# The overflow loop of an expert stage moved to the middle of the experts, and four reorderings in the r/k/v stage

## What is computed

```python
xs = cols + (prev - cols) * rwkv_mu            # r, k, v and three low-rank inputs
kk = (k * k_k) / max(norm of each head of (k * k_k), 1e-12)
k  = k * (1.0 + (a - 1.0) * k_a)
g  = sigmoid(g_d) @ g_lora_up                  # g_d: 128 of the columns
bonus = sum over a head of (r * k * r_k), times v
...
grp = argmax(x2d @ router_group + router_group_bias)
top_v, top_i = top_k(expert scores inside the group, 2)
for e in range(N_EXPERTS):                     # 32 experts, D_EXPERT = 256
    h = silu(x2d @ moe_w_gate[e]) * (x2d @ moe_w_up[e])
    y = y + combine[:, e:e + 1] * (h @ moe_w_down[e])
y = rms_norm(x + y)
```

## Time and profile before

| | us |
|---|---|
| median of 3 runs | 1114.06 |
| lowest, highest | 1112.53, 1117.73 |
| the profiled execution | 1116.11 |
| its span, first to last instruction | 1114.4 |

### The profile page before, as it was taken

How to read it: one execution, slowest core, us unless ns; L and a number is a source line. 1 busy time by engine, 2 the same in 40 slices (tenths; PEclk the granted TensorE clock), 3 DMA queues, 4 the chain that set the end, 5 groups by cost and what they waited for, 6 DMA issues and landing times. The chain is left out here.

```text
span 1114.4 us, 24781 instructions
## 1 busy us (share of the span) xinstructions
PE 1014.4 (91%) x10429; PEld 768.3 (69%) x10429; DVE 566.8 (51%) x1195; ACT 365.2 (33%) x783; POOL 442.8 (40%) x458
## 2 busy tenths in 40 slices
PE   5999999789999999999999999999976999888784
PEld 5777777578888887888888888884554555454441
DVE  6577777556565643777645446333363222211126
ACT  3444544545545443444244450000111111110112
POOL 7646546244554424977653335410001222211110
PEclk9999999899999999999999999999987999988998
DMA  8022221110000007541242224407786999999975
GB/s 257 18 78 73 69 81 38 37 47 4 4 5 4 4 4 190 164 112 37 63 143 85 76 66 161 151 1 288 318 338 223 414 415 414 415 418 416 416 293 229
DMA packets 84935, 183.11 MB, mean 164 GB/s; under 512 B 9921, under 2 KB 59613, under 8 KB 76122
## 3 DMA queue, kind: packets, MB, share of 16 engines
q1 hardware_dynamic: 78173, 168.59, 41.6%
q0 software_dynamic: 5168, 8.56, 2.1%
q10 hardware_dynamic: 1485, 4.39, 1.0%
HBM read 173.24 MB, written 17.55 MB: 171 GB/s over the span
## 5 line engine op out<-in xcount | busy, mean ns | idle before, releaser
L2802 DVE SCALAR_TENSOR_TENSOR ex_sg<-tl_psA,ex_slot_rs,ex_sg 128x128 f32<-128x128 f32 x32 | 11.2, 351 | 138.3 <-ACT ex_sg L2602 138.1
L2294 POOL DMA_INDIRECT d_y<-tl_xn,ex_sidx x32 | 31.9, 998 | 118.6 <-DVE tl_xn L2806 108.5
L2289 POOL DMA_INDIRECT tl_xn<-d_tok,ex_gidx x17 | 17.9, 1051 | 148.4 <-DVEq L2794 76.4
L262 PE MATMUL psv<-xT,w_sum 128*128 128x260 f32 x256 | 61.6, 384 | 0.9 <-DVE uv_gu L1595 0.6
L224 POOL TENSOR_TENSOR w_sum<-w 128x512 f32<-128x512 f32 x16 | 21.2, 1324 | 94.0 <-PE mg_w L262 93.8
L262 PEld LDWEIGHTS psv<-xT,w_sum 128*128 128x128 f32 x256 | 48.4, 190 | 9.4 <-issue 1.0
L2602 ACT ACTIVATE ex_sg<-tl_psA,ex_slot_rs 128x128 f32<-128x128 f32 x32 | 11.8, 368 | 130.9 <-PE tl_psA L2460 130.9
L1058 PE MATMUL ck_b<-ck_X,ck_V 64*64 64x64 f32 x1280 | 50.4, 222 | 4.1 <-issue 3.3
L262 PE MATMUL rk_ps<-xT,rk_w 128*128 128x260 f32 x208 | 50.1, 384 | 0.0
L262 PE MATMUL rk_ps<-xS,rk_w 128*128 128x260 f32 x200 | 48.6, 386 | 0.0
L1058 PEld LDWEIGHTS ck_b<-ck_X,ck_V 64*64 64x64 f32 x1280 | 43.0, 134 | 4.5 <-issue 4.2
(11 more groups left out here) (615 smaller groups left out, 2795.2 us busy)
## 6 DMA issues: line engine op xcount, KB each, us to landing
wd<-in_moe_w_down SPq DMA_DIRECT2D x15, 1024.0 KB, 23.4
rk_w<-in_w_in SPq DMA_DIRECT2D x12, 1024.0 KB, 5.5
tl_x<-in_moe_w_down SPq DMA_DIRECT2D x9, 1024.0 KB
w_uv<-in_w_in SPq DMA_DIRECT2D x16, 512.0 KB, 5.2
w<-in_w_in SPq DMA_DIRECT2D x8, 1024.0 KB, 5.8
xT<-in_moe_w_gate SPq DMA_DIRECT2D x5, 1024.0 KB
xT<-in_moe_w_up SPq DMA_DIRECT2D x5, 1024.0 KB
bonus_all<-in_moe_w_gate SPq DMA_DIRECT2D x5, 1024.0 KB
```

Source lines behind the costliest of these rows:

```text
L262: ins = eng.matmul(bank[:, 0:TH], w[:, k, :], x[:, k, :], start=(first and k == 0), stop=(last and k == NK // 2 - 1), skip_group_check=True)
L2289: eng.indirect_dma_start(out=xg[:, p % 2, :], out_offset=None, in_=m.d_tok, in_offset=bass.IndirectOffsetOnAxis(ap=gidx[:, p:p + 1], axis= ...
L2294: eng.indirect_dma_start(out=m.d_y2, out_offset=bass.IndirectOffsetOnAxis(ap=rows, axis=0), in_=yo[:, x, :], in_offset=None, bounds_check= ...
L2802: eng.scalar_tensor_tensor(out=sg[:, out, :], in0=psg[out][:, P:2 * P], scalar=scale, in1=sg[:, out, :], op0=ALU.mult, op1=ALU.mult).then_ ...
```

## The change

In the r/k/v stage: (a) on VectorE the second `shift_mix` stands behind `u2(0)` instead of ahead of it; the tanh for `gate_in` stands behind `decays(1)` on ScalarE, the affine step of `gate_in` behind the weight sums of set 1 on GpSimd, and `keys(1)` waits for the tanh. (b) In the last set `head_sums(7)` stand behind the fourth product, `products(7)` ahead of `norms(6)`, `norms(7)` ahead of `c22`. (c) `roots(6)` stands behind `logs(7)`. (d) `scaled(6)` stands behind `c21`.

In the expert stage the loop stands at position 21 of 32 and has max number + 1 passes: its first pass is expert 31, the others are the overflow blocks. The positions are: 0 to 19 experts 0 to 19, position 20 expert 30, position 21 the loop, positions 22 to 31 experts 20 to 29. The loop's slot is 21 % 7 = 0. It has its own semaphores (`l_...`). The list of gathers is written in six instructions instead of two, because the pairs are no longer in the order of the experts.

```diff
-SPARE = 26 % SLOTS
+MID = 21
+SPARE = MID % SLOTS
 # GpSimd, r/k/v
-            eng.wait_ge(s_lt, 1)
-            eng.tensor_scalar(m.gate_in[:, :], m.gate_in[:, :], 0.5, 0.5, ALU.mult, ALU.add).then_inc(s_lt, 1)
-            eng.wait_ge(s_lt, 2)
...
                 weight_sums(eng, rkv_blocks(m, w, s), s_wsum, 4 * s)
+                if s == 1:
+                    eng.wait_ge(s_lt, 1)
+                    eng.tensor_scalar(m.gate_in[:, :], m.gate_in[:, :], 0.5, 0.5, ALU.mult, ALU.add).then_inc(s_lt, 1)
 # TensorE, r/k/v
-                if s % 3 == 2 and s < RKV_SETS - 1:
-                    head_sums(p)
+                if s % 3 == 2:
+                    head_sums(p if s < RKV_SETS - 1 else p + 1)
...
                 product(eng, bank_w, b.t1, x.s1, last=False).then_inc(s_prod, 1)
...
-                if s % 3 == 2:
+                if s % 3 == 2 and s < RKV_SETS - 1:
                     head_sums(p + 1)
 # ScalarE, r/k/v
                 decays(p + 1)
+                if i == 0:
+                    eng.wait_ge(s_xs, 2)
+                    eng.activation(m.gate_in[:, :], xs[:, 1, :], ACT.Tanh, scale=0.5).then_inc(s_lt, 1)
...
                 logs(p)
-                if i == NP // 2 - 1:
-                    roots(p)
                 kept_sums(p + 1)
                 logs(p + 1)
-                if i < NP // 2 - 1:
-                    roots(p)
+                roots(p)
                 roots(p + 1)
 # VectorE, r/k/v
                 u2(s)
+                if i == 0:
+                    low_rank_rows(1)
...
                 received(p + 1)
+                products(p + 1)
                 if i == NP // 2 - 1:
                     norms(p)
-                products(p + 1)
                 u3(s + 2)
+                norms(p + 1 if i == NP // 2 - 1 else p)
+                c22(s + 2)
                 if i < NP // 2 - 1:
-                    norms(p)
-                c22(s + 2)
-                norms(p + 1)
-                if i == NP // 2 - 1:
-                    scaled(p)
+                    norms(p + 1)
                 c21(s + 2)
             p, s = NP - 2, RKV_SETS - 1
+            scaled(p)
             c12(s)
             scaled(p + 1)
 # experts
+def counted(k):
+    return k if k <= MID else k - 1
+def expert_at(k):
+    return k if k < MID - 1 else k + NE - MID - 1 if k <= MID else k - 2
+def loads_at(k):
+    return k // SLOTS + (0 if k > MID and (k - MID) % SLOTS == 0 else 1)
 # SP
+            def load_block(k):
+                if k == MID + SLOTS:
+                    eng.wait_ge(l_over, 1)
+                else:
+                    eng.wait_ge(s_gu, counted(k - SLOTS) + 1)
+                load_gate_up(eng, m, a, k % SLOTS, expert_at(k))
+                if k != MID + SLOTS:
+                    eng.wait_ge(s_down, counted(k - SLOTS) + 1)
+                load_down(eng, m, a, k % SLOTS, expert_at(k))
+
+            for k in range(SLOTS, MID):
+                load_block(k)
             n = passes(eng)
             with eng.Fori(0, n) as q:
                 e = eng.value_load(m.block_expert[0:1, bass.ds(q, 1)], min_val=0, max_val=NE - 1)
                 eng.wait_ge(s_gu_free, q + 1)
-                load_gate_up(eng, m, a, SPARE, e)
+                load_gate_up(eng, m, a, SPARE, e, l_wgu)
                 eng.wait_ge(s_d_free, q + 1)
-                load_down(eng, m, a, SPARE, e)
+                load_down(eng, m, a, SPARE, e, l_wd)
+            for k in range(MID + 1, NE):
+                load_block(k)
 # TensorE
+                eng.wait_ge(l_wgu, q * 32 + 32)
+                gate_up(SPARE, 0, halves_of[1], 1, l_gu)
+                eng.wait_ge(l_h, q + 1)
+                turn_h(1, l_ht)
+                eng.wait_ge(l_hte, q + 1)
+                eng.wait_ge(l_wd, q * 16 + 16)
+                down(SPARE, 1, l_down)
+                eng.wait_ge(l_in, q * 16 + 16)
+                turn(0, l_t)
+                eng.wait_ge(l_yo, q + 1)
+                eng.wait_ge(l_xgT, q * 2 + 2)
+            up_block(MID + 1)
+            up_block(MID + 2, MID // 2 + 2, MID + 1)
+            for k in range(MID + 3, NE):
+                up_block(k, k // 2 + 1 if k % 2 == 0 and k + 2 < NE else None, k - 1)
+            down_block(NE - 1)
 # ScalarE: s_gu_free
+                if k == MID - SLOTS:
+                    eng.sem_inc(s_gu_free, 1)
...
+                silu(1, rs_now[:, 0:1], l_sg)
                 eng.sem_inc(s_gu_free, 1)
 # VectorE: gather list and number of passes
             for h, rows in enumerate(halves_of):
-                step.did(eng.tensor_scalar(gidx[rows, 0:NE // 2], lists[rows, h::2], float(EMPTY), None, ALU.add))
+                for pairs, first, count in ((slice(0, MID // 2), h, MID // 2), (slice(MID // 2, MID // 2 + 1), NE - 2 + h, 1),
+                                            (slice(MID // 2 + 1, NE // 2), MID - 1 + h, NE // 2 - MID // 2 - 1)):
+                    step.did(eng.tensor_scalar(gidx[rows, pairs], lists[rows, first:first + 2 * count - 1:2], float(EMPTY), None,
+                                               ALU.add))
...
-                do(eng.tensor_scalar(m.passes[:, 0:1], end[:, NE - 1:NE], 1.0, None, ALU.max))
+                do(eng.tensor_scalar(m.passes[:, 0:1], end[:, NE - 1:NE], 1.0, None, ALU.add))
```

More of the change, by code:

```diff
@@ L739, in _, with low_rank_rows @@
             step.wait()
-            for n in range(2):
+            def low_rank_rows(n):
                 eng.wait_ge(s_le, n + 1)
@@ L2453, in turn, with gate_up @@
                                          m.ident[:, :])
-                last.then_inc(s_t, 1)
-            def gate_up(x, at, slots_of, out):
+                last.then_inc(done, 1)
+            def gate_up(x, at, slots_of, out, done=s_gu):
                 w = m.wgu[x].rearrange("p n k (h f) -> p k n h f", h=2)
@@ L2461, in gate_up, with turn_h, down @@
                                           xgT[:, at, kk, slots_of], w[:, kk, :, h, :], start=(kk == 0), stop=(kk == NK - 1))
[L2462 to L2467 removed]
+                last.then_inc(done, 1)
+            def turn_h(out, done=s_ht):
+                eng.transpose(psh[:, 0:P], sg[:, out, :], m.ident[:, :]).then_inc(done, 1)
+            def down(x, out, done=s_down):
                 for kk in range(DE // P):
@@ L2471, in down @@
                                           start=(kk == 0), stop=(kk == DE // P - 1))
-                last.then_inc(s_down, 1)
+                last.then_inc(done, 1)
             def turn_pair(p):
@@ L2873, in _ @@
             weights()
-            for k in range(NE):
-                eng.wait_ge(s_sg, k + 1)
-                product(k % 2, slot_rs[:, k:k + 1])
-                if k % 2 == 0:
-                    eng.wait_ge(s_t, k // 2 + 2)
-                    rows((k // 2 + 1) % 2)
+            for k in range(MID):
+                dve_block(k, k // 2 + 1 if k % 2 == 0 else None)
                 if k:
@@ L2887, in _ @@
                     extra_indices()
-            result_block(NE - 1)
+            result_block(MID - 1)
+            n = passes(eng)
+            with eng.Fori(0, n) as q:
+                eng.tensor_copy(rs_now[:, :], slot_rs[:, bass.ds(q + (NE - 1), 1)])
+                eng.tensor_copy(gidx_now[:, :], xidx[:, bass.ds(q, 1)]).then_inc(l_now, 1)
+                eng.wait_ge(l_now, q * 2 + 1)
+                eng.wait_ge(l_sg, q + 1)
+                product(1, rs_now[:, 0:1], l_h)
+                eng.wait_ge(l_down, q + 1)
+                eng.wait_ge(s_y[1], q * 16 + MID // 2 * 16)
+                eng.tensor_copy(sidx_now[:, :], sidx[:, bass.ds(q + (NE - 1), 1)]).then_inc(l_now, 1)
+                result(1, l_yo)
+                eng.sem_inc(s_d_free, 1)
+                eng.wait_ge(l_t, q + 1)
+                rows(0, l_xgT)
+            eng.sem_inc(l_over, 1)
+            dve_block(MID + 1)
+            dve_block(MID + 2, MID // 2 + 2)
+            result_block(MID + 1)
+            for k in range(MID + 3, NE):
+                dve_block(k, k // 2 + 1 if k % 2 == 0 and k + 2 < NE else None)
+                result_block(k - 1, n)
+            result_block(NE - 1, n)
             for d, j in enumerate((0, 2)):
```

265 lines of the change are left out of this document (130 added, 135 removed).

## The result

The changed kernel takes 1127.24 us (median of 4 runs), beside 1115.89 us for the kernel before on the same chip: ratio 1.0092, 95% interval 1.0063 to 1.0121, so 7 to 13.5 us slower. Forecast were +6.0 us on 1114.06, so 1120.1, with 1125 as the upper end. The direction and the larger cause (the hole) were right; the size was too small, for what the change does to the end of the kernel was not in the sum.

A forecast was written before the change was run, and what follows sets the result against it. From about block 18 on, the stream of weights was taken as the bound, TensorE before. Terms -1.6 + 0.8 + 0.6 + 5.7 + 0.3 + 0.2 = +6.0 us on 1114.06 gave 1120.1 us; 8-in-10 range 1115.5 to 1125.

The forecast's parts named there:

- the hole: Expert loop: SP waits for pass 0's SiLU before loading more, so the weights' stream runs dry 6.0 us; +5.7 us net.
- Start and end of r/k/v: r/k/v stage: TensorE's wait for u2(0) goes, -1.6 us; GpSimd's late work on pair 6 sets the end, +0.8 us.
- the prediction's estimate by it: Expert loop: by the skill's DMA cost, pass 1's weights arrive in 6.8 us, not 7.2, taking 0.4 us off the hole.
- The sign that was named: Expert loop: DMA busy share near 0 for some 6 us at about 986 to 993 us.
- rival 3: SP's loop exit or pass 1's down load comes late, a second gap in the stream; 2 to 6 us more, chance 0.15.
- Rivals 1 and 2: Experts: 1, stream has slack, gap doesn't show, 1114.4 us, chance 0.13; 2, overflow list empty, 1106.4 us, chance 0.05.
- The list: Between router and first gather: four more instructions for the list of gathers, +0.6 us, bounds 0.3 to 0.8.
- Experts: start and end: Expert stage's two ends: +0.6 us for the list of gathers, then +0.3 and +0.2 us at the last block.
- The last block is now an ordinary one: End of experts: last gate_up to last scatter takes 9.47 us as for block 31, not 9.15; +0.3 us.
- some +0.2 more: Last scatter to SP's read: 22 tokens instead of 5 cost +0.2 us, range 0 to 0.6.
- a bound for the hole: Expert loop: upper bound 9 us, with gate_up at the lower clock, 5.36 us, and SP needing 1.5 us.

The follow-up runs named there:

- e3: Changed kernel with position 22's weights issued by SP between those of pass 0 and pass 1; 1.0019 of the kernel before.
- e12: Changed kernel with experts 29 and 21 changed over, so the last block carries 51 tokens; trace only, no ratio, 3.71 us from last scatter to SP's read.
- e8: Kernel before with only parts (b), (c), (d) of the r/k/v change; trace only, no ratio, stage-end barrier at 218.98 us instead of 218.01.
- e9: Changed kernel with 2 idle products ahead of the last gate_up and 6 ahead of the first combining; 1.0053 of the kernel before.
- e5: Changed kernel with 4 idle products ahead of the last gate_up and 11 ahead of the first combining; 1.0099 of the kernel before.
- e4: Changed kernel with the number of passes one higher, the third pass over an empty list; 1.0213 of the kernel before.

## Why the prediction was wrong in size

- **Start and end of r/k/v**: right. -1.7 for -1.6, +1.0 for +0.8, with GpSimd as the last engine and two table loads instead of four, as said.
- **The hole**: right in cause and place, and in size within 1 us. With all forecast times moved by the 2.3 us that this trace is ahead, pass 0's `gate_up` was to begin at 984.5 and SP to issue at 988.9; measured are 983.50 and 987.39. Of these 1.5 us, 1.0 are the `gate_up`'s, and the rest comes because SP issues 0.22 us behind the SiLU's start (987.17) and not behind its end. The rate is back above 400 GB/s in the slice from 989.5, 2.1 us behind the issue, for 1.9 in the forecast. (The Trainium skill, DMA: Bandwidth & Descriptors, Anatomy of one DMA, has about 2.0 us per DMA that don't go with the bytes, for DMAs that GpSimd issues, and most of it for the completion. The 2.1 us here run from an issue of SP until the rate is up, so the trace doesn't bear the page's figure out, and the prediction's estimate by it carried it over to another path.) So the hole's end came earlier than forecast, and what made up for that was the taper ahead of it, which the forecast, with a sharp start at 984.7, did not have. Forecast 5.7; filling gives 5.6 to 6.0 back from first to last `gate_up`, and the traces of the two kernels differ by 6.6. The sign that was named, a DMA share near 0 for some 6 us, did not come for the same reason: it is 0.46 from 984 to 990. No second hole: the DMA share from 990 to 1000 is 1.02, rival 3 falls. Rivals 1 and 2 fall by e3 and by the two passes.
- **The list**: +0.3, the lower bound that was given, for the narrow instructions are shorter (0.66 us for six).
- **The step that failed: "Experts: start and end", the end.** "The last block is now an ordinary one" was costed at +0.3 by comparing it with block 31, and "some +0.2 more" for 22 tokens. Nothing was added from SP's read on. Measured are +4.7 for the 0.5 forecast, and three terms that were not in the sum make up the difference. (1) +1.7: the last `gate_up` runs at the lower clock (0.67). In the kernel before, the loop's rows were turned (1.09 us) behind the `gate_up` of block 30, TensorE then idled 1.15 us ahead of block 31, and the last block was the loop's, which began without a wait, its weights long in. Now the last blocks have no pair left to turn, TensorE idles 2.61 us for the last weights, and 32 products take 5.36 us instead of 3.67. The comparison took the duration of block 31 without what kept TensorE busy in front of it. (2) +1.2 from SP's read to the end, mostly the combining at 5.25 us (0.70) instead of 3.70, behind 6.02 us of idling instead of 1.82. The residual's copies stand ahead of it in both kernels. But the loop's last turn, which used to hold them back, is gone, so they start 0.21 us behind the scatter's issue instead of 1.27; they take 3.83 us together instead of 5.28, for in the kernel before they ran at the lower clock themselves (0.53); and SP's read comes 1.4 us later. Over the six traces of the new order without products there, the stretch from SP's read to the end is 29.25 to 30.79 us, against 28.30 to 28.44 in four of the old. I had followed the scatter, not what the moved loop left empty on TensorE. (3) +1.4 from the scatter to SP's read, with the packet of code in its window (mean over the traces 1.1); the rows' share is 0.05. That this term is the change's is not shown.
- Neither (1) nor (2) comes every time. e12, of the new order, has its last `gate_up` at the full clock. e8, whose experts are those of the kernel before, ran its copies at 1.88 us each, then idled 3.43 us and combined at the lower clock, and its stretch from SP's read is 29.42 us:

```profile
1095.29 5.40 PE L2536 MATMUL tl_psA<-xT,spare 128*128 128x512 f32 x8 [3.43 <-DMA xT<-d_y]
```

- The warning for (1) and (2) stood in the trace of before: 3.54 us of idling with a `gate_up` of 5.32 us behind it. I used that duration as a bound for the hole and not for the end.
- **The base**: 1114.06 was the median of three runs; in the later comparisons the kernel before has 1115.9 to 1117.0. That is 2 us of the 7 by which the time was missed, 3.0 (9.0 - 6.0) are the ledger's: 4.2 from the end and 0.9 from the hole, less the 1.8 us of luck in the unchanged stretch and 0.3 from the list. The rest, 2.3 us, lies between the two traces and the medians.

## What to carry to other kernels

When a loop is moved, price what it leaves behind as carefully as what it meets: here the loop's turn and its ready block left the end of the kernel, TensorE idled longer there, and the lower clock behind the idling cost 2.9 us in this pair of traces, half as much as the hole that was forecast. Where a queue in order has to wait for one slot, first issue the loads whose slots are free: one load ahead of the waiting one took the hole back. Idle products that hold the clock pay only where they end about when the data arrive: some tenths too late still paid (e9), over 3 us did not (e5).

## What was not expected of the hardware

- The level of TensorE's clock behind a gap is not a function of the gap alone: `gate_up` ran at 5.36 us behind 2.22 us of idling (e9, at 1053.17) and at 3.67 behind 2.47 (e12, at 1079.10). At the first combining the two sides parted cleanly: 3.70 us behind 1.43 to 1.94 us of idling (four traces), 5.19 to 6.71 behind 1.99 to 6.02 (eight traces).
- A 16 KB packet of code on one of the 16 DMA engines goes with 1.1 us more between a small scatter and the engine that waits for it. The scatter's rows land as early as without it; the waiting engine goes on 1.12 to 1.23 us behind the packet's end (ten traces).
- A DMA stream with a deep queue ends in a taper of some 10 us, one with a short queue within 3 us; the bytes lost are nearly the same (in e4's rates the two holes are worth 7.4 and 7.1 us of 414 GB/s).
- A stretch of 627 us, from the r/k/v barrier to the first expert, varied by 8 us from trace to trace though at most the list differs in it, more than most terms of the sum: for terms of 1 us the stretch in the trace decides, the time of the kernel can't.
